# The experts' down weights with two neighbouring rows in each partition

## What is computed

```python
def swiglu(h, wg, wu, wd):
    return (jax.nn.silu(h @ wg) * (h @ wu)) @ wd

def moe(h, w_router, w_gate, w_up, w_down):
    ...                      # combine: (tokens, 8), two nonzero weights in each row
    for e in range(N_EXPERTS):
        y = y + combine[..., e:e + 1] * swiglu(h, w_gate[e], w_up[e], w_down[e])
    return y
```

## Time and profile before

| | |
|---|---|
| Median of 3 runs | 1716.27 us (1710.91 to 1716.49) |
| Span of the profiled execution | 1714.8 us |
| TensorE busy (matmuls) | 1637.2 us, 95% |
| TensorE weight loads, beside them | 1037.3 us |
| VectorE, ScalarE, GpSimd busy | 428.6, 278.3, 115.6 us |
| Mean granted TensorE clock | 0.971 |
| DMA | 462.96 MB, mean 270 GB/s |
| DMA in the experts' stage (from about 1000 us) | 376 to 397 GB/s in the slices of the page |

### The profile page before, as it was taken

One profiled execution on the slowest core, in us unless ns is written; L12 is line 12 of the kernel. 1 busy time (PEld: TensorE's weight loads), 2 busy tenths in 40 slices (PEclk: granted clock), 3 DMA queues, 4 the chain that ended last, 5 costly groups with the idle time before them and its releaser, 6 DMA issues.

```text
span 1714.8 us, 20876 instructions
## 1 busy us (share of the span) xinstructions
PE 1637.2 (95%) x8068; PEld 1037.3 (60%) x8068; DVE 428.6 (25%) x992; ACT 278.3 (16%) x621; POOL 115.6 (7%) x195
## 2 busy tenths in 40 slices
PE   6999998899999999998899999999999999999998
PEld 3554554478888878877787544554445454544444
DVE  2233332230000035679567200010000100010113
ACT  2122222220000022346513100000000000000001
POOL 0000404200000010020010200000000100010000
PEclk9999899999999999988899999999999999999999
DMA  9755884244433563544359899999999999999998
GB/s 356 262 185 203 274 293 118 86 141 148 147 117 120 165 224 114 160 137 153 89 197 368 305 334 388 386 381 389 380 397 382 381 377 392 386 376 395 391 384 318
DMA packets 255195, 462.96 MB, mean 270 GB/s; under 512 B 13454, under 2 KB 112811, under 8 KB 251989
## 3 DMA queue, kind: packets, MB, share of 16 engines
q1 hardware_dynamic: 240544, 413.94, 67.7%
q0 software_dynamic: 12048, 46.53, 8.2%
q10 hardware_dynamic: 2512, 1.23, 0.3%
HBM read 445.97 MB, written 15.88 MB: 269 GB/s over the span
## 4 chain that ended last, share of the span: by engine, by line
PE 86%; DVE 7%; DMA 2%; issue 2%; ACT 2%; SPq 1%; POOLq 0%; POOL 0%; DVEq 0%; ACTq 0%
PE bank L1365 18%; PE bank L1052 9%; PE bank L1406 9%; PE bank L1380 9%; PE bank L1022 8%; PE bank L1418 5%; PE bank L1066 5%; PE bank L761 3%; PE bank L1100 2%; PE bank L851 1%; PE bank L798 1%; DMA st<-in_state_ssm 1%; PE bank L769 1%; PE bank L1168 1%; PE bank L856 1%
## 5 line engine op out<-in xcount | busy, mean ns | idle before, releaser
L1365 PE MATMUL bank<-ring,hg 128*128 128x512 f32 (+1 forms) x624 | 251.8, 560 | 0.7 <-ACT hg L1697 0.7
L1365 PEld LDWEIGHTS bank<-ring,hg 128*128 128x128 f32 x624 | 118.0, 190 | 130.1 <-issue 127.7
L1052 PE MATMUL bank<-hT,ring 128*128 128x264 f32 x704 | 156.9, 386 | 0.3 <-ACT hT L1477 0.3
L1052 PEld LDWEIGHTS bank<-hT,ring 128*128 128x128 f32 x704 | 133.7, 190 | 23.4 <-issue 0.6
L2317 DVE TENSOR_TENSOR actH<-sgH,bank 128x512 f32<-128x512 f32 (+1 forms) x24 | 15.4, 643 | 455.4 <-PE bank L1365 455.4
L1022 PE MATMUL bank<-hT,ring 128*128 128x264 f32 x512 | 118.6, 393 | 1.6 <-ACT hT L1477 1.3
L1406 PE MATMUL bank<-ring,turnH 128*128 128x512 f32 x256 | 114.3, 599 | 3.3 <-ACT turnH L1722 3.3
L1022 PEld LDWEIGHTS bank<-hT,ring 128*128 128x128 f32 x512 | 99.0, 194 | 19.9 <-issue 2.1
L1380 PE MATMUL bank<-ringx,hg 128*64 128x256 f32 x832 | 93.0, 381 | 0.0
L1406 PEld LDWEIGHTS bank<-ring,turnH 128*128 128x128 f32 x256 | 47.2, 190 | 67.8 <-issue 66.9
L1066 PE MATMUL bank<-actT,ring 128*128 128x264 f32 x352 | 79.1, 386 | 0.6 <-DVE actT L1934 0.6
(11 more groups left out here) (528 smaller groups left out, 1833.4 us busy)
## 6 DMA issues: line engine op xcount, KB each, us to landing
ring<-in_moe_w_down SPq DMA_DIRECT2D x70, 1024.0 KB, 13.3
ring<-in_moe_w_up SPq DMA_DIRECT2D x59, 1024.0 KB, 11.8
ring<-in_moe_w_gate SPq DMA_DIRECT2D x55, 1024.0 KB, 12.1
ring<-in_w_ada SPq DMA_DIRECT2D x48, 1024.0 KB, 9.1
ringx<-in_moe_w_gate SPq DMA_DIRECT2D x37, 1024.0 KB, 11.6
ringx<-in_moe_w_up SPq DMA_DIRECT2D x33, 1024.0 KB, 12.8
ring<-in_ssm_w_in SPq DMA_DIRECT2D x20, 1024.0 KB, 5.3
ringx<-in_moe_w_down SPq DMA_DIRECT2D x20, 1024.0 KB, 12.7
```

Of the source, the lines that this page charges most:

```text
L1052: m = mm(bank[2 * w + q][:, 0:T], slot8(tl)[:, k, q * P:(q + 1) * P], hT[:, k, :], start=k == 0, stop=k == DC - 1)
L1365: m = mm(bank[b_][:, 0:width], hg[:, k, 0:CAPH], w[:, kk, :], start=k == 0, stop=k == DC - 1)
```

## The change

The down weights are viewed as `e (b p q) n -> e p b (q n)`: hidden row 256 b + 2 p + q. A tile is one b, so partition p gets the neighbouring rows 256 b + 2 p and 256 b + 2 p + 1, one run of 2048 floats. Size, number and order of the DMAs stay.

Row chunk q of a down tile now holds the hidden columns 256 b + 2 p + q, so the turned activations must have them in that order. The heavy expert's transposes take every second column of a block of 256 in `actH`, once the even and once the odd ones. The light expert gets its order from gate and up: `v_` 0 takes the even and `v_` 1 the odd columns of each block of 256, so the streamed weights are read with a step of two floats. All other instructions stay as they are.

```diff
--- before.py
+++ after.py
@@ -427,7 +427,7 @@
     wout_d = a["ssm_w_out"][0].rearrange("(c p) n -> p c n", p=P)
     mg = a["moe_w_gate"][0].rearrange("e (c p) n -> e p c n", p=P)
     mu = a["moe_w_up"][0].rearrange("e (c p) n -> e p c n", p=P)
-    md = a["moe_w_down"][0].rearrange("e (c p) n -> e p c n", p=P)
+    md = a["moe_w_down"][0].rearrange("e (b p q) n -> e p b (q n)", p=P, q=2)
     DOWN_K = [(0, 6), (6, 6), (12, 5), (17, 5)]
 
     def moe_slot(t):
@@ -528,7 +528,7 @@
             t = MOE_AT[tile]
             f0, width = GROUPS[g]
             if kind == "down":
-                src, rows = md[ds(e, 1), :, 4 * g + 2 * i:4 * g + 2 * i + 2, :], 2
+                src, rows = md[ds(e, 1), :, 2 * g + i:2 * g + i + 1, :], 1
             else:
                 rows = SLOT // width
                 src = (mg if kind == "gate" else mu)[ds(e, 1), :, rows * i:rows * (i + 1), f0:f0 + width]
@@ -1373,7 +1373,7 @@
                     pe.wait_ge(s["moe_act"], acted("light", g - 1) if g else n * (2 * NG) + 2)
                     for b_, kind in enumerate(("gate", "up")):
                         for i in range(DC // rows):
-                            w = weights("light", kind, g, i).rearrange("p k (u v f) -> p k v u f", v=2, f=P)
+                            w = weights("light", kind, g, i).rearrange("p k (u f v) -> p k v u f", v=2, f=P)
                             for kk in range(rows):
                                 k = rows * i + kk
                                 for v_ in range(2):
@@ -1385,7 +1385,8 @@
                     pe.wait_ge(s["moe_act"], acted("heavy", g))
                     pe.wait_ge(s["moe_copied"], turns_before("heavy", g))
                     for q in range(GROUPS[g][1] // P):
-                        m = pe.transpose(bank[3][:, q * P:(q + 1) * P], actH[:, q * P:(q + 1) * P], ident)
+                        rows = actH[:, 2 * P * (q // 2):2 * P * (q // 2 + 1)].rearrange("p (f q) -> p q f", q=2)[:, q % 2, :]
+                        m = pe.transpose(bank[3][:, q * P:(q + 1) * P], rows, ident)
                     m.then_inc(s["moe_turned"], 1)
 
                 def light_turn(g):
```

## The result

The changed kernel takes 1727.01 us (median of 7 runs, 1723.89 to 1728.93) against 1716.27 us before (7 runs, 1710.91 to 1721.94): a ratio of 1.0062 with a 95% interval of 1.004 to 1.0083, that is 7 to 14 us slower. I had forecast 1716 and no change. The time lies inside my range, but on the side of the rival that I gave 0.16.

What follows compares the result with a forecast made beforehand. The prediction took the kernel to be bound by TensorE's matmuls, transfers a close second. All terms were 0, so the span stayed 1714.8 us and the forecast median was 1716 us, range 1706 to 1740.

Steps and rivals of the forecast that it cites:

- What bounds the kernel: Experts' stage: TensorE's matmuls bind end to end, 32.24 us a group, with transfers a close second.
- (1) the DMA: Down-weight tiles in 8 KB runs: some 7 us less DMA time, hidden beside matmuls, so worth 0.
- One sign that I had named: SP's waits for TensorE, 238.8 us for line 1365 alone, were to stay as before.
- (2) the light matmuls: Light gate and up, line 1380, reading weights at every second float: same length, 0; upper end 146 us.
- My upper end, 146 us: Light gate and up: cost if the two instructions of a pair no longer run beside each other.
- (3) the heavy transposes: Line 1388, 88 weight loads taking actH at a step of two floats: 0; upper end 12.3 us.
- A: Rival: the step slows TensorE in light gate and up or the heavy transposes, 1728 to 1862 us; chance 0.16.
- B: Rival: 8 KB runs move worse than 4 KB ones and transfers become the bound, up to 1766 us; chance 0.04.
- C: Rival: transfers bound more than the waits show, so the change is faster, at best 1703 us; chance 0.05.
- D: Rival: 8 KB runs are cut into two 4 KB packets again; 1716 us, included in the forecast's 0.75.

Runs made afterwards that it cites:

- VectorE: As a run: the full change against the kernel before, but VectorE writes the even/odd order, the step staying only in the light short groups; 1717.46 us, ratio 1.0009.

## Why the prediction was wrong

- *What bounds the kernel*: right. The chain was TensorE end to end and stayed so. With no slack in it each longer instruction appears in the time.
- *(1) the DMA, 0*: right, and its sizes too: I worked out 423 GB/s; the window shows 422. The transfers alone gave 1.0003, and a stage of the same length. One sign that I had named failed: SyncE's waits for TensorE did not stay as before, they grew, since the slots did not come free any sooner.
- *(2) the light matmuls, 0*: this step failed. The term is 7.4 us. I argued that a stream takes one float each second cycle and so has room. The share lost, 4.8%, is the same in a stream alone, so the room that I inferred from the pace isn't there. My upper end, 146 us, was the loss of the pair's overlap; no run showed that mechanism, and a loss of this size appears only at a step of four floats.
- *The rule that I weighed there*, from the Trainium skill's page "SBUF — State Buffer", section "Door 1: The DMA port swizzle": lines of 16 bytes, full rate with two accesses in a line. The runs agree that the cliff lies beyond two floats of a line (7.40 against 14.57 us). They disagree with "full": two floats a line cost 4.8%. The same section says how far one can "stride for free", for this type "4 fp32"; read as a step of four, that is contradicted by the 14.57 us. The measurement decides.
- *(3) the heavy transposes, 0 "for the reason of (2)"*: failed too, by 2.3 us. I had written that the weight load sets the pace of these four (148 ns each); that too was only partly so, for a load grew by 69 ns, from 140 to 209, and a transpose in the chain by 22, from 148 to 170. Since steps of two and four cost the same there, the reason isn't that of (2) either.
- *The rivals*: A was the case. I had written that 0.5% needs a loss of 5.5% on line 1380. The 4.8% and the transposes together, 9.7 us, are 0.57% of the time, and the measured median is 10.7 us higher. I gave A 0.16 because no row priced a step; both ends of the cost reached upwards alone, and a cost with no cover and no gain possible deserved more than that. B, C and D are refuted: landings are shorter and TensorE waits for no tile (B), the transfers alone leave the stage at 753.75 us (C), and the packets are of 8 KB (D).
- *Not foreseen*: the clock's falls between pairs. They explain 2.6 us between the two traces. Whether the change makes them more frequent stays open: with the gathers in one piece, all seven traces with a step in light gate and up or in the heavy transposes had two light down products of 4.7 to 6.2 us, the three without such a step (before, transfers only, VectorE) had one, the one with a step in heavy gate and up none, but a fall behind the first heavy transposes. The pattern is regular, but one look at each kernel shows no cause. The runs of the kernel with the transposes' step alone were 6.2 us slower in the mean; its stage in the one trace is 3.6 longer, falls included. The rest, 2.6 us with a standard error of 1.3, goes with a lower mean clock (0.9716 against 0.9743); where it lies is not shown.

## What to carry to other kernels

Where the chain is one engine without a gap, an access pattern with a step has to be priced before a wider DMA run is bought with it: the transfer's gain was hidden and the step's price was not. If an order has to be changed, give it to the engine with slack, here VectorE, whose product of 128 x 512 took as long with a step as without. On TensorE a step of two floats cost some 5% of the stream; a step of four doubled the time of a pair of streams. And where only one stage of a kernel is touched, compare that stage's length in the traces: here the whole kernel's runs spread over 17 us, and two stages with the same code on TensorE agreed to 0.01.

## What the runs showed of the hardware

- TensorE's streamed float32 operand: 429 ns for 512 columns from a block, 450 at a step of two floats. For a pair of streams, 64 instructions of 256 columns in 7.06, 7.40, 14.57 and 14.88 us at a step of one, two, four and eight floats.
- TensorE's weight load of 128 x 128 float32 in a transpose: 140 ns from a block, 209 at a step of two, 212 at a step of four.
- VectorE's float32 product of 128 x 512 with SBUF and PSUM inputs: 687 ns from blocks, 688 at a step of two floats.
- HBM to SBUF, in windows of 2 us of two traces: 386 GB/s in runs of 2 KB, 410 of 4 KB, 422 of 8 KB.
- The granted clock fell to 1.2 GHz behind 3.7 us of transposes in some of the seams and not in others of the same trace; with 1.8 us of them at a time it fell in none of nine seams in three traces. A fall made the 3.58 us of a light down product 4.7 to 6.2.
